# A two-block, two-layer transformer kernel in split fp32: pooled branch rounded at once, carried input in the tail, another opening

## The reference

```python
# first block, per layer
x = x + 0.5 * rmsnorm(swiglu(rmsnorm(x, w1), w_gu, w_down), w2)      # ffn1
z = rmsnorm(x, w3) @ w_in                                            # mixer: differential attention,
x = x + rmsnorm(merged(attention(z), mlstm(z)) @ w_out, w4)          #   mLSTM, gates
x = x + 0.5 * rmsnorm(swiglu(rmsnorm(x, w5), w_gu, w_down), w6)      # ffn2
# second block, per layer
y = concat(attention_a, attention_b, spatial_gating, multiscale_pool) @ w_o
x = layer_norm(ALPHA * x + y)
y = (silu(conv(gate)) * conv(val)) @ w_down                          # conv FFN, width 2816
x = layer_norm(ALPHA * x + y)
```

## Time and profile before

| | us |
|---|---|
| median of 3 runs | 2027.77 |
| lowest, highest | 2026.53, 2047.41 |
| the profiled execution, its own time | 2028.39 |
| span of that execution | 2026.6 |
| TensorE busy | 1991.6 |
| VectorE, ScalarE busy | 1266.2, 1100.1 |
| moved by DMA | 335.87 MB, 166 GB/s |

### The profile page before, as it was taken

One profiled execution on the slowest core, in us unless ns is written; L12 is line 12 of the kernel. 1 busy time (PEld: TensorE's weight loads), 2 busy tenths in 40 slices (PEclk: granted clock), 3 DMA queues, 4 the chain that ended last, 5 costly groups with the idle time before them and its releaser, 6 DMA issues.

```text
span 2026.6 us, 29957 instructions
## 1 busy us (share of the span) xinstructions
PE 1991.6 (98%) x11872; PEld 1744.1 (86%) x11872; DVE 1266.2 (62%) x2132; ACT 1100.1 (54%) x1713; POOL 6.5 (0%) x17
## 2 busy tenths in 40 slices
PE   7999999999999999999999999999999999999998
PEld 6888898999888888879989988888889997889997
DVE  5555777566555655567856765558467776647675
ACT  5444676465544654466754664446355556536554
POOL 0000000000000000000000000000000000000000
PEclk9999999999999999999999999999899999989999
DMA  7666445544666566545454556664335665325553
GB/s 254 190 188 186 148 138 174 158 146 157 214 187 188 151 200 189 187 153 159 139 184 136 157 203 188 187 186 136 94 116 178 185 184 167 115 84 173 176 183 92
DMA packets 93691, 335.87 MB, mean 166 GB/s; under 512 B 10224, under 2 KB 12528, under 8 KB 93552
## 3 DMA queue, kind: packets, MB, share of 16 engines
q1 hardware_dynamic: 92256, 328.59, 52.1%
q0 software_dynamic: 720, 4.44, 0.6%
q10 hardware_dynamic: 576, 0.92, 0.1%
HBM read 332.86 MB, written 1.05 MB: 165 GB/s over the span
## 4 chain that ended last, share of the span: by engine, by line
PE 93%; DVE 4%; ACT 2%; issue 1%; DMA 0%; SPq 0%; DVEq 0%; ACTq 0%
PE stream L1731 11%; PE stream L1732 10%; PE stream L1733 10%; PE stream L1737 9%; PE stream L1739 9%; PE stream L1738 9%; PE acc L1737 8%; PE acc L1738 8%; PE acc L1739 8%; DVE w_lo L1027 1%; PE stream L1827 1%; PE acc L2266 1%; ACT w_hi L535 1%; PE acc L2127 1%; PE stream L1788 1%
## 5 line engine op out<-in xcount | busy, mean ns | idle before, releaser
L1027 DVE TENSOR_TENSOR w_lo<-w_raw,w_hi 128x1024 fp32r<-128x1024 f32 x624 | 760.8, 1223 | 417.6 <-ACT w_hi L535 416.9
L535 ACT ACTIVATE w_hi<-w_raw 128x1024 fp32r<-128x1024 f32 x624 | 655.5, 1055 | 441.9 <-PE stream L1739 208.3
L1731 PE MATMUL stream<-h_hi,w_hi 128*128 128x256 f32 (+1 forms) x1504 | 434.3, 289 | 2.7 <-DVE h_lo L1426 2.7
L1733 PE MATMUL stream<-h_hi,w_lo 128*128 128x256 f32 (+1 forms) x1504 | 424.8, 282 | 0.0
L1732 PE MATMUL stream<-h_lo,w_hi 128*128 128x256 f32 (+1 forms) x1504 | 424.7, 282 | 0.0
L1737 PE MATMUL stream<-w_hi,h_hi 128*128 128x512 f32 x864 | 342.4, 396 | 2.2 <-DVE h_lo L1426 2.2
L1739 PE MATMUL stream<-w_lo,h_hi 128*128 128x512 f32 x864 | 337.3, 390 | 0.0
L1738 PE MATMUL stream<-w_hi,h_lo 128*128 128x512 f32 x864 | 337.0, 390 | 0.0
L1731 PEld LDWEIGHTS stream<-h_hi,w_hi 128*128 128x128 f32 x1504 | 287.9, 191 | 10.5 <-issue 7.1
L1732 PEld LDWEIGHTS stream<-h_lo,w_hi 128*128 128x128 f32 x1504 | 288.1, 192 | 0.8
L1733 PEld LDWEIGHTS stream<-h_hi,w_lo 128*128 128x128 f32 x1504 | 287.8, 191 | 0.0
(11 more groups left out here) (302 smaller groups left out, 2309.1 us busy)
## 6 DMA issues: line engine op xcount, KB each, us to landing
w_raw<-in_w_up SPq DMA_DIRECT2D x264, 512.0 KB, 3.7
w_raw<-in_w_mix SPq DMA_DIRECT2D x228, 512.0 KB, 3.7
w_raw<-in_w_down SPq DMA_DIRECT2D x132, 512.0 KB, 3.7
params<-in_params POOLq DMA_DIRECT2D x4, 859.5 KB, 5.5
out_x<-x_residual SPq DMA_DIRECT2D x4, 256.0 KB, 2.6
constants<-in_consts POOLq DMA_DIRECT2D x1, 896.0 KB, 6.4
x_residual<-in_x ACTq DMA_DIRECT2D x3, 256.0 KB, 4.2
x_residual<-in_x SPq DMA_DIRECT2D x1, 256.0 KB, 4.3
```

The costliest lines, as they stand in the source:

```text
L535: nc.scalar.activation(w_hi[:, u % RING], w_raw[:, u % RAW], ACT.Copy).then_inc(hi_ready, 1)
L1027: nc.vector.tensor_tensor(w_lo[:, u % RING], w_raw[:, u % RAW], w_hi[:, u % RING].bitcast(F32), ALU.subtract).then_inc(split_done, 1)
L1731: nc.tensor.matmul(dst, w_hi[:, s, w], hi, start=first, stop=False)
L1733: return nc.tensor.matmul(dst, w_lo[:, s, w], hi, start=False, stop=last)
```

## The change

- Opening: ScalarE's queue issues the gains and then its three quarters of x, and 384 instead of 256 columns of constants (ones, ones, identity). ScalarE rounds x by quarters in 128x256 pieces, two and then a `w_hi`, four times; VectorE does the same with `h_lo` and `w_lo`. TensorE runs both halves for each unit of the first chunk. Before it, TensorE runs six fp32 products of 512 columns on a cleared tile, which nobody reads.
- The rest of the constants and the mixer parameters are loaded by POOL only when `w_raw` slot 2 has been filled three times; the wait for constants ahead of the first `turn_chunk` is gone.
- Mixer start: `pre_sum` of half 1 moves from the end of the FFN to behind the mixer's second `lo_next`, `prepare` to behind its third.
- Pooled branch: `d_round` before `take_values`; `d_rest` at i = 17 instead of 18.
- `carry` of half 1 moves out of `mixer2` and of the down units into `tail_norm`, between half 0 and half 1.
- Left statistics: the last unit signals its left 512 columns (`acc_left`), and VectorE forms their `bn_stats` before it waits for the rest. ScalarE's Ln waits for `bn_aggr` (`ln_stat`) only, and `ln_shift` for the negated mean (`ln_centre`).

The diff with its context cut; left out are the two new semaphores and index changes for `feed_lo`.

```diff
@@ -254,6 +254,12 @@
 
+        def hi_act_at(fd):
+            return 0 if fd == 0 else KT + (fd - 1) * (KT + KT // 2)
+
+        def lo_at(fd, t, k):
+            return k + 1 if fd == 0 else KT + (fd - 1) * 2 * KT + t * KT + k + 1
+
         def feed_gain(fd, k):
@@ -457,7 +465,6 @@
         def _(sp):
-            sp.dma_start(gn[:], gains).then_inc(gains_in, 16)
             sp.dma_start(xr[:, 0:2], x[:, 0:2]).then_inc(x_in[0], 16)
@@ -537,10 +544,7 @@
                 for k in range(KT if t else KT // 2):
-                    if fd == 0:
-                        act.wait_ge(x_in[k // 2], 16)
-                    else:
-                        act.wait_ge(x_ready, (fd - 1) * 16 + t * KT + k + 1)
+                    act.wait_ge(x_ready, (fd - 1) * 16 + t * KT + k + 1)
                     nc.scalar.activation(dst[:, k, half(t)], xr[:, k, half(t)], ACT.Identity,
@@ -816,6 +820,7 @@
                                          scale=-0.5).then_inc(post_rs, 1)
+                    act.wait_ge(ln_centre, 2 * e + t + 1)
                     act.wait_ge(post_rs, 2 * n + t + 1)
@@ -967,29 +972,30 @@
                     if i == V_C1 + 3:
+                        d_round()
                         take_values(0)
                         take_values(1)
-                        d_round()
                     if i == OUT_TURN_AT:
...
 
+            act.dma_start(gn[:], gains).then_inc(gains_in, 16)
             for q in range(1, 4):
                 act.dma_start(xr[:, 2 * q:2 * q + 2], x[:, 2 * q:2 * q + 2]).then_inc(x_in[q], 16)
-            act.dma_start(cst[:, 0:2 * P], consts[:, 0:2 * P]).then_inc(ones_in, 16)
+            act.dma_start(cst[:, 0:3 * P], consts[:, 0:3 * P]).then_inc(ones_in, 16)
             exp_set()
-            act.wait_ge(init, 3)
+            act.wait_ge(init, 4)
             act.wait_ge(gains_in, 16)
-            feed(0, 0)
-            hi_next()
-            hi_next()
-            feed(0, 1)
-            hi_next()
+            for q in range(4):
+                act.wait_ge(x_in[q], 16)
+                for k in (2 * q, 2 * q + 1):
+                    nc.scalar.activation(h_hi[:, k], xr[:, k], ACT.Identity,
+                                         scale=feed_gain(0, k)).then_inc(feed_hi_act, 1)
+                hi_next()
             for t in range(QT):
                 pre_square(0, t)
-            for s in range(AHEAD - 3):
-                hi_next()
+            hi_next()
             for l in range(DEPTH):
@@ -1033,9 +1039,9 @@
                 if t == 0 and k >= KT // 2:
-                    dve.wait_ge(feed_hi, fd * (KT // 2) + k - KT // 2 + 1)
+                    dve.wait_ge(feed_hi, (fd - 1) * (KT // 2) + k - KT // 2 + 1)
                 else:
-                    dve.wait_ge(feed_hi_act, fd * (KT + KT // 2) + t * (KT // 2) + k + 1)
+                    dve.wait_ge(feed_hi_act, hi_act_at(fd) + t * (KT // 2) + k + 1)
                 hi, lo = feed_tiles(fd)
@@ -1078,8 +1084,6 @@
                 lo_next()
-                if fd % 3 == 1:
-                    pre_sum(fd, 1)
 
@@ -1329,9 +1333,12 @@
 
-                prepare()
                 for j in range(8):
                     lo_next()
+                    if j == 1:
+                        pre_sum(n, 1)
+                    if j == 2:
+                        prepare()
                 dve.wait_ge(pre_rs, n + 1)
@@ -1393,18 +1400,18 @@
                 def statistics(t):
+                    dve.wait_ge(acc_left, 2 * e + t + 1)
+                    nc.vector.bn_stats(st6[:, t, 0], acc_tok[t][:, 0:512])
                     if t == 0:
...
                         dve.wait_ge(unit_done, last + 1)
-                    for q in range(2):
-                        r = nc.vector.bn_stats(st6[:, t, q], acc_tok[t][:, q * 512:(q + 1) * 512])
-                    r.then_inc(dve_step, 1)
+                    nc.vector.bn_stats(st6[:, t, 1], acc_tok[t][:, 512:D]).then_inc(dve_step, 1)
                     dve.wait_ge(dve_step, stepped())
-                    nc.vector.bn_aggr(mvar[:, t], st6[:, t].rearrange("p q s -> p (q s)")).then_inc(dve_step, 1)
-                    dve.wait_ge(dve_step, stepped())
+                    nc.vector.bn_aggr(mvar[:, t], st6[:, t].rearrange("p q s -> p (q s)")).then_inc(ln_stat, 1)
+                    dve.wait_ge(ln_stat, 2 * e + t + 1)
                     nc.vector.tensor_scalar(nmean[:, t:t + 1], mvar[:, t, 0:1], -1.0, None,
-                                            ALU.mult).then_inc(ln_stat, 1)
+                                            ALU.mult).then_inc(ln_centre, 1)
 
@@ -1638,7 +1645,7 @@
                         window_sums(1)
-                    if i == V_C1 + 4:
+                    if i == V_C1 + 3:
                         d_rest()
@@ -1648,25 +1655,19 @@
 
+            nc.vector.memset(y_tok[:, 0, 0:512], 0.0).then_inc(init, 1)
             nc.vector.memset(eps1[:], EPS).then_inc(init, 1)
...
             dve.wait_ge(gains_in, 16)
-            for k in range(KT // 2):
-                feed_lo_dve(0, 0, k)
-            lo_next()
-            for k in range(KT // 2, KT):
-                dve.wait_ge(x_in[k // 2], 16)
-                feed_hi_dve(0, 0, k)
-                if k > KT // 2:
-                    feed_lo_dve(0, 0, k - 1)
-            feed_lo_dve(0, 0, KT - 1)
-            lo_next()
-            lo_next()
-            for k in range(KT):
-                feed_lo_dve(0, 1, k)
-            lo_next()
+            for q in range(4):
+                for k in (2 * q, 2 * q + 1):
+                    dve.wait_ge(feed_hi_act, k + 1)
+                    nc.vector.scalar_tensor_tensor(out=h_lo[:, k], in0=xr[:, k], scalar=feed_gain(0, k),
+                                                   in1=h_hi[:, k].bitcast(F32), op0=ALU.mult,
+                                                   op1=ALU.subtract).then_inc(feed_lo, 1)
+                lo_next()
             lo_next()
@@ -1693,8 +1694,8 @@
 
-            pool.wait_ge(raw_full[2], 16)
-            pool.dma_start(cst[:, 2 * P:], consts[:, 2 * P:]).then_inc(consts_in, 16)
+            pool.wait_ge(raw_full[2], 3 * 16)
+            pool.dma_start(cst[:, 3 * P:], consts[:, 3 * P:]).then_inc(consts_in, 16)
             pool.wait_ge(ones_in, 16)
@@ -1783,6 +1784,8 @@
                 def squares(t, k):
+                    if n == 0 and t == 0 and k == 0:
+                        pe.wait_ge(ones_in, 16)
                     if k == 0:
@@ -1794,7 +1797,7 @@
                         if c == 0:
-                            pe.wait_ge(feed_lo, n * 16 + t * KT + k + 1)
+                            pe.wait_ge(feed_lo, lo_at(n, t, k))
                         r = tokens((side if c == 0 else bank)[t][:], h_hi[:, k, half(t)], h_lo[:, k, half(t)], u,
@@ -1816,8 +1819,6 @@
                     pe.wait_ge(chunk_gated, (f * CHUNKS + c) * 2 + 2)
-                    if c == 0:
-                        pe.wait_ge(consts_in, 16)
                     if c == 1:
@@ -1845,13 +1846,19 @@
 
-                for t in range(QT):
+                if n == 0:
                     for j in range(4):
-                        if t == 0:
-                            if j == 2 and n > 0:
-                                turn(n - 1, 1)
-                            unit(u0 + j)
-                        up(0, j, t)
+                        unit(j)
+                        for t in range(QT):
+                            up(0, j, t)
+                else:
+                    for t in range(QT):
+                        for j in range(4):
+                            if t == 0:
+                                if j == 2:
+                                    turn(n - 1, 1)
+                                unit(u0 + j)
+                            up(0, j, t)
                 both(1, 0, 0)
@@ -2129,12 +2136,19 @@
                 for t in range(QT):
+                    if t == 1:
+                        for k in range(KT):
+                            carry(t, k)
                     for i, u in enumerate(units):
...
                         hi, lo = operand(u)
-                        r = wide_rows(u, hi, lo, t, False, i == len(units) - 1)
+                        last = i == len(units) - 1
+                        r = tokens(acc_tok[t][:, 0:512], hi[:, half(t)], lo[:, half(t)], u, slice(0, 512), False, last)
+                        if last:
+                            r.then_inc(acc_left, 1)
+                        r = tokens(acc_tok[t][:, 512:D], hi[:, half(t)], lo[:, half(t)], u, slice(512, D), False, last)
                         if t == 1:
@@ -2361,12 +2374,13 @@
                         if i == VALUES_AT:
-                            for t in range(QT):
-                                for k in range(KT):
-                                    carry(t, k)
+                            for k in range(KT):
+                                carry(0, k)
                 tail_norm(2 * l, tuple(u0 + U_MIX2 - LAG + j for j in range(LAG)), mixed, arrived)
 
```

(11 more changed lines are left out.)

3 lines of the change are left out of this document (1 added, 2 removed).

## The result

| us | before | after |
|---|---|---|
| median | 2027.3 (of 4: 2026.53, 2026.83, 2027.77, 2047.41) | 2004.06 (of 4: 2003.57, 2003.91, 2004.2, 2009.19) |
| span of the profiled execution, its own time | 2026.6, 2028.39 | 2001.7, 2003.57 |
| TensorE busy | 1991.6 | 1983.4 |
| waits of TensorE for `w_lo`, opening and mixers | 13.9 | none listed |

The ratio is 0.9851, with a 95% interval of 0.9802 to 0.99. The forecast was 2005.5. The executions of the kernel before fall into two groups of times, near 2027 and from 2040 to 2048; what parts them is taken up in the experiments.

What follows compares the result with a forecast made beforehand. TensorE was taken as the bound, with a product in flight in 1991.6 of 2026.6 us. Savings of 4.9 + 2.2 + 3.6 + 11.2 + 0.6 = 22.5 gave 2005.9, taken as 2005.5 us; range 2003 to 2009.

Steps and rivals of the forecast that it cites:

- Opening: First chunk: warm-up and both halves per unit bring chunk 1's first product from 25.97 to 21.1, saving 4.9 us.
- upper bound of 5.4: Most the opening could save, in us, if the weights came half a microsecond earlier.
- Mixer parameters: Mixer start: sums and parameters made later, so TensorE's waits of 1.37 and 0.84 go, saving 2.2 us (1.8 to 2.5).
- Pooled branch: Ahead of the value products: earlier rounding removes both `ya_lo` waits, saving 3.6 us (at least 3.0).
- The clock behind it: Value products in both layers: without the gap the clock stays up, saving 6.4 + 4.8 = 11.2 us (zero to 11.2).
- The rival that the small products alone bring the clock down: Value products: 48 load-bound records suffice without a gap; waits gone, slow stretches kept, time 2017; chance 0.12.
- Layer norm: Layer norms: negated mean off the path, 0.2 at the end and small gains in gaps, saving 0.6 us (0 to 1.5).
- How the numbers follow: Chances: forecast 0.50, one fall 0.24, small products 0.12, opening 0.08, both fall 0.06; 0.52 between faster and slower by 1%.
- the first rival: Conv layers: clock falls behind a layer-norm gap, 192 products of 128 columns slow, costing 19 us; time 2025; chance 0.24.
- an opening that gives nothing: Opening: warm-up too late or first loads later in their new order, 4.9 us lost; time 2010.5; chance 0.08.
- both falls: Both conv layers: the clock falls at each, 39 us, time 2044.5, or 2055.7 with slow value products; chance 0.06.

Runs made afterwards that it cites:

- a_sp: Kernel after, with the gains issued by SyncE ahead of x again instead of by ScalarE: 2005.47, 2006.47, 2024.13, 2024.37 us.
- b_pool: Kernel before with only the pooled-branch part of the change (pooled halves rounded ahead of the value tiles, their rest one unit sooner): median 2017.92 us, ratio 0.9909.
- a_pool: Kernel after with the pooled-branch part undone (rounding behind both value tiles, rest at unit 18): median 2019.86 us of ten, in two groups.
- a_drest: Kernel after with only the rest of the pooled halves (`d_rest`) put back at unit 18: median 2026.73 us of ten.
- a_noleft: Kernel after with both statistics of a half formed only once the whole half is there: median 2004.16 us of six.
- b_turn1: Kernel before with only the turn of half 0 one unit earlier in the four tails: median 2027.88 us of twelve, ratio 0.9965.
- a_nowarm: Kernel after without the six warm-up products: median 2025.3 us of four (2006.13, 2025.03, 2025.56, 2025.9).
- a_warm8: Kernel after with eight warm-up products instead of six: 2006.12, 2006.2, 2006.4, 2010.49, 2025.54, 2025.69 us.
- a_tfirst: Kernel after with the first chunk in the old order, all of half 0 over four units, then half 1: 2005.48, 2011.04, 2025.39, 2025.54 us.
- a_turn1: Kernel after with the turn of half 0 one unit earlier, behind the second tail unit of half 1: 1998.43 to 2000.31 us, ratio 0.9797.
- a_best: a_turn1 plus, at the layer norm between the layers, half 1's statistics and `y_tok` ahead of a `w_lo`: median 1997.74 us, ratio 0.9802.
- a_gap: Kernel after with a VectorE memset lengthening TensorE's gap ahead of conv layer 0: 2010.72, 2012.32, 2012.76, 2027.21 us.

## Why the prediction was right, and where it was wrong

The sum was right, the weighing was not.

*Opening.* Forecast 4.9, measured 6.1. The products are 0.23 apart, no unit but the first is waited for, and the clock is up, as argued. The first product came at 8.55, not 10.1: I let the loads in their new order give nothing, and a_sp shows that taking the gains out of SyncE's queue brings the first weights 1.3 earlier. That puts this pair of traces above even my upper bound of 5.4; against b_pool's 25.02, the same opening as before, it would be 5.2. Taken one by one, the order of halves is worth 1.9, the warm-up 2.1, the gains 1.1, each from one pair of traces. No wait of TensorE for POOL's late constants or parameters is listed.

*Mixer parameters.* Forecast 2.2, measured 2.6: both waits are gone, and each took about 0.2 more with it than its row says. Most of that is in how the row counts: idle time begins at the modelled end of the last product, 0.39 after its start, while products that follow each other are 0.23 apart. The part was not tried alone.

*Pooled branch.* Forecast 3.6, measured 4.0, again 0.2 per wait. The second value tile is last now, two microseconds before it is wanted, as said.

*The clock behind it.* Forecast 11.2, measured 11.4, carry 8.13 behind the start against a forecast of 8.2. The rival that the small products alone bring the clock down is refuted by the kernel after and b_pool; that the gap is needed is shown from both sides by b_pool and by layer 0 of a_pool. What I did not see is that the gap is not enough: behind 1.05 us (a_drest) and behind 1.78 us (a_pool) the clock fell in layer 0 and stayed up in layer 1. That both stretches were slow in the profiled execution of before, so that the whole 11.2 could be had back, is partly luck of that execution.

*Layer norm.* Forecast 0.6, measured 0.8 in all, by difference. The wait at the end is 0.2 shorter (3.5 to 3.3), as said. The left statistics carry 0.1 of it (a_noleft).

*What failed* is the step "How the numbers follow", and in it the first rival. I had its mechanism, its place and its price right: a fall behind the gap of 1.3 ahead of 192 products of 128 columns, 19 us. But I put it on the kernel after alone, "against it: neither gap did so in this trace", although one of the three times of before lay 19.6 above the median, and took 2027.77 for what the kernel before costs. The runs show that the price of this fall is in 32 of 57 executions of the kernel before (b_turn1 takes it away) and in none of ten of the kernel after. So the case that I priced at 2025, "within 1%", would have stood against a before that is itself above 2040 in most executions. With the 0.24 of that case, the 0.12 of the small products, the 0.08 of an opening that gives nothing, 0.05 of the forecast and 0.03 of both falls on "within 1%", the chances said 0.52 for no difference that can be told; the sum that I trusted for the time said faster, and the measured ratio is 0.9851, clear of 1. That the compared median of before was 2027.3 is luck as well: three of its four executions were of the lower group. Against the median of the 57, 2040.8, the kernel after is 37 us faster.

*Open*: why the kernel after is spared. A shift of 1.1 to 2.3 us ahead of everything (a_nowarm, a_warm8, a_tfirst, a_sp) brings the price of the long fall into nine of eighteen executions, with the same gap of 1.25, against none of sixteen without a shift (the ten, and a_noleft's six). The phase against something that the kernel does not set would do it; no run shows what that is, and whether a shift of another size would be safe was not tried. Nor was any variant run on two chips; the kernel before has both groups of times on each of the four chips that it ran on beside the variants, so the chip alone does not decide. So the kernel after was lucky in its place, while a_turn1 and a_best need no luck with the long fall.

## What to carry to other kernels

Before forecasting, explain the spread of the times: one time of three that lies the price of a known mechanism above the others is that mechanism, in the kernel before. Look at the granted clock behind each short wait of TensorE, most of all where narrow products follow (64 or 128 columns, 0.11 apart, with the weight load busy nearly all the time): here a wait of 1 us cost up to 5 at the value products and up to 20 at a conv layer. And close such a gap by putting work behind the producer's trigger: the turn one unit earlier closed it and gave 4 us, while the earlier statistics, which speed up the producer, gave 0.1.

## What the runs showed of the hardware that I had not expected

- A gap of 1.05 us of TensorE was followed by a stretch at 0.61 of the clock once and at 1.00 once, in one execution (a_drest); so was a gap of 1.78 (a_pool). The one traced gap of 2.85 was followed by the lower level at once (a_gap).
- Once down, TensorE, with products of 128 columns 0.21 apart and never idle, stayed at the lower level for 41 us in a_nowarm, but came back after about 14 in a_gap and about ten in b_pool.
- A shift of the whole kernel by 1.1 to 2.3 us changed how often the long fall, some 1450 us later, occurred: from none of sixteen to nine of eighteen.
- One small DMA ahead of x on SyncE's queue made the first weights usable at 7.4 to 7.7 us instead of 6.0 to 6.5.
